# Routing of a two-level mixture of experts on one core: the first pair's weight slots released in two halves, logits in one operation, places read straight from TensorE's ranks, counts taken apart

## The reference, cut to what matters

```python
h = rmsnorm(x, g_ffn)
lg = h @ w_rg + b_rg                      # 4 group logits
g_onehot = one_hot(argmax(lg), 4)
le = (h @ w_re).reshape(..., 4, 8) + b_re # 32 expert logits
le_sel = sum(le * g_onehot[..., None], axis=-2)
tv, ti = top_k(le_sel, 2)                 # 2 of the 8 experts of the chosen group
gate = p_top * softmax(tv)                # spread over the 32 experts
for e in range(32):
    hid = silu(h @ w_e1[e]) * (h @ w_e3[e])   # 1024 -> 256
    y = y + gate[..., e:e+1] * (hid @ w_e2[e])  # 256 -> 1024
x = x + y
```

## Time and profile before

| what | us |
|---|---|
| time, median of 3 runs (lowest, highest) | 663.09 (662.82, 663.72) |
| time of the profiled execution | 663.22 |
| its span in the trace | 661.4 |
| TensorE busy | 621.0 |
| VectorE busy | 331.7 |
| ScalarE busy | 170.2 |
| GpSimd busy | 152.1 |

### The profile page before, as it was taken

How to read it: one execution, slowest core, us unless ns; L and a number is a source line. 1 busy time by engine, 2 the same in 40 slices (tenths; PEclk the granted TensorE clock), 3 DMA queues, 4 the chain that set the end, 5 groups by cost and what they waited for, 6 DMA issues and landing times.

```text
span 661.4 us, 9857 instructions
## 1 busy us (share of the span) xinstructions
PE 621.0 (94%) x3662; PEld 381.5 (58%) x3662; DVE 331.7 (50%) x878; ACT 170.2 (26%) x540; POOL 152.1 (23%) x341
## 2 busy tenths in 40 slices
PE   6999999999989889999999999997999999987886
PEld 5678876676545557776677756854344343333341
DVE  2162765878787997721123331477236335333333
ACT  4425223421558513232110001111121120120200
POOL 1497445733477963000000000000000000000000
PEclk9899999999999899999999999999999999997997
DMA  9763472221401072031289994077999999999993
GB/s 284 177 216 129 160 231 95 65 65 28 162 0 33 1 254 75 23 113 47 97 250 370 407 367 159 1 293 317 416 415 416 415 417 418 416 417 417 416 408 115
DMA packets 61681, 150.55 MB, mean 228 GB/s; under 512 B 12352, under 2 KB 40448, under 8 KB 53696
## 3 DMA queue, kind: packets, MB, share of 16 engines
q1 hardware_dynamic: 61632, 149.89, 61.2%
HBM read 147.12 MB, written 2.76 MB: 227 GB/s over the span
## 4 chain that ended last, share of the span: by engine, by line
PE 51%; DVE 7%; SPq 3%; DMA 3%; issue 2%; POOL 2%; ACT 1%; DVEq 0%
PE PS L811 18%; PE PS L1178 7%; PE PS L1087 6%; PE PS L819 5%; PE PS L1217 4%; PE PS L1207 4%; DMA E<-in_w_e 3%; SPq L700 3%; PE PS L932 1%; PE PS L955 1%; DVE X L2070 1%; PE PS L1139 1%; PE PS L1060 1%; SPq L704 1%; DVE rotB L1688 1%
## 5 line engine op out<-in xcount | busy, mean ns | idle before, releaser
L811 PE MATMUL PS<-hT,W 128*128 128x320 f32 x448 | 128.4, 442 | 1.1 <-issue 1.1
L811 PEld LDWEIGHTS PS<-hT,W 128*128 128x128 f32 x448 | 85.2, 193 | 39.0 <-issue 7.3
L1178 PE MATMUL PS<-E,xT 128*32 128x256 f32 x1024 | 61.5, 393 | 8.2 <-issue 7.2
L2142 POOL TENSOR_SCALAR means<-sums 128x4 f32<-128x4 f32 (+3 forms) x35 | 7.9, 227 | 224.5 <-ACT junk L1315 223.0
L1178 PEld LDWEIGHTS PS<-E,xT 128*32 128x32 f32 x1024 | 36.3, 114 | 37.6 <-issue 22.0
L1087 PE MATMUL PS<-h,S 128*128 128x512 f32 (+1 forms) x96 | 48.2, 625 | 0.7 <-DVE S L1929 0.7
L1217 PE MATMUL PS<-yb,WG 128*128 128x512 f32 (+1 forms) x96 | 42.8, 654 | 4.0 <-DVE X L2070 3.1
L819 PE MATMUL PS<-W,hT 128*128 128x256 f32 (+5 forms) x256 | 41.8, 353 | 1.6 <-ACT memT L1297 1.6
L2070 DVE TENSOR_TENSOR X<-X,PS 128x512 f32<-128x512 f32 (+1 forms) x48 | 33.0, 687 | 10.2 <-PE PS L1217 8.6
L819 PEld LDWEIGHTS PS<-W,hT 128*128 128x128 f32 (+1 forms) x256 | 31.5, 163 | 10.2 <-ACT memT L1297 1.8
L819 PE MATMUL PS<-W,mergedT 128*128 128x384 f32 (+3 forms) x192 | 35.8, 382 | 1.6 <-DVE mergedT L1838 1.6
(11 more groups left out here) (313 smaller groups left out, 952.4 us busy)
## 6 DMA issues: line engine op xcount, KB each, us to landing
E<-in_w_e SPq DMA_DIRECT2D x93, 1024.0 KB, 21.8
W<-in_w_in SPq DMA_DIRECT2D x7, 1536.0 KB, 7.3
W<-in_w_in SPq DMA_DIRECT2D x7, 1024.0 KB, 9.3
W<-in_w_mem_kv SPq DMA_DIRECT2D x4, 1024.0 KB, 6.0
W<-in_w_glu SPq DMA_DIRECT2D x4, 768.0 KB, 7.4
W<-in_w_out SPq DMA_DIRECT2D x2, 1536.0 KB, 14.8
E<-in_w_e SPq DMA_DIRECT2D x6, 512.0 KB, 18.8
X<-in_x_prompt SPq DMA_DIRECT2D x4, 512.0 KB, 5.2
```

The source lines that it names most:

```text
L811: ins = mm(out[:, 0:TOK], w[:, k, cols:cols + 128], rhs[:, k, :], start=(k == 0), stop=(k == kt - 1))
L1178: ins = mm(PS[r:r + B, 2 + par, 0:FF], xT[:, k, place_ + B * n:place_ + B * n + B], E13[slot][:, :, k, 128 * j:128 * j + 128], start=(k == ...
L2142: link(g_.tensor_scalar(means[0:rows_, n, 0:heads], sums[0:rows_, n, 0:heads], 1.0 / NORM_WIDTH[key[0]], EPS, ALU.mult, ALU.add))
```

## The change

Four edits.

1. **The weight slots of the first pair.** The loads of experts 7 and 8 are cut into halves over k. The first halves (k 0 to 3, 4 DMAs of 512 KB) are issued when `up(0)` has finished its step k = 3 (`first_half`), the second halves (4 more of 512 KB) at `ab_full`. `up` waits for both.
2. **Logits in one operation.** The router's columns are laid experts first, then groups, so that one operation writes 36 logits in place of two (4 and 32).
3. **Places straight from TensorE.** Each rank product gets a further product, `ones` of 32 rows by `iota`, which adds 32 times the expert's number. What `of_expert` picks is then already the place. `homes` goes from three small operations to two; the bound 32 times the expert plus 32 is computed in `experts`, and the plain rank is restored later by one operation ahead of `jcmp`.
4. **Counts apart.** The experts' counts are no longer accumulated beside the last ranks. `last_ranks` ends after one product, and three products into another bank follow (`counted`); VectorE copies them after the second half of `normed(2)`.

```diff
-            for p in range(PAIRS):
-                if 2 * p + UPS < NE:
+            for k0 in (0, KD // 2):
+                sp.wait_ge(s["first_half"] if k0 == 0 else s["ab_full"], 1)
+                for e in range(2):
+                    for n in range(2):
+                        sp.dma_start(E13[e][:, n, k0:k0 + KD // 2, :], e13_src[n][:, e + UPS, k0:k0 + KD // 2, :])\
+                            .then_inc(up_loaded[e] if k0 == 0 else s[f"rest{e}_loaded"], 16)
+            for p in range(PAIRS):
+                if p > 0 and 2 * p + UPS < NE:
...
             def first_ranks():
-                mm(PS[:, YB, 0:NE], const("upper"), both[:, 0, :], start=True, stop=True).then_inc(s["rank_full"], 1)
+                mm(PS[:, YB, 0:NE], const("ones", B), const("iota", B)[:, 0:NE], start=True, stop=False)
+                mm(PS[:, YB, 0:NE], const("upper"), both[:, 0, :], start=False, stop=True).then_inc(s["rank_full"], 1)
 
             def next_ranks():
-                mm(PS[:, YB, NE:2 * NE], const("upper"), both[:, 1, :], start=True, stop=False)
+                mm(PS[:, YB, NE:2 * NE], const("ones", B), const("iota", B)[:, 0:NE], start=True, stop=False)
+                mm(PS[:, YB, NE:2 * NE], const("upper"), both[:, 1, :], start=False, stop=False)
                 mm(PS[:, YB, NE:2 * NE], const("ones"), both[:, 0, :], start=False, stop=True).then_inc(s["rank_full"], 1)
                 for t in range(NT - 1):
-                    mm(PS[:, LAST_RANKS, 0:2 * NE], const("ones"), both[:, t:t + 1, :].broadcast_to([128, 2, NE]), start=(t == 0), stop=False)
+                    mm(PS[:, LAST_RANKS, 0:NE], const("ones"), both[:, t, :], start=(t == 0), stop=False)
+                mm(PS[:, LAST_RANKS, 0:NE], const("ones", B), const("iota", B)[:, 0:NE], start=False, stop=False)
 
             def last_ranks():
-                mm(PS[:, LAST_RANKS, 0:NE], const("upper", DEC), both[0:DEC, 2, :], start=False, stop=False)
-                mm(PS[:, LAST_RANKS, NE:2 * NE], const("ones", DEC), both[0:DEC, 2, :], start=False, stop=True).then_inc(s["rank_full"], 1)
+                mm(PS[:, LAST_RANKS, 0:NE], const("upper", DEC), both[0:DEC, 2, :], start=False, stop=True).then_inc(s["rank_full"], 1)
+                for t, (f, n) in enumerate(TILES):
+                    ins = mm(PS[:, YB, 0:NE], const("ones", n), both[0:n, t, :], start=(t == 0), stop=(t == NT - 1))
+                ins.then_inc(s["counted"], 1)
...
-                st.mark(V_.scalar_tensor_tensor(lg[0:n, t, 0:NG], src[0:n, 0:NG], r, brow[0:n, 0:NG], ALU.mult, ALU.add))
-                link(V_.scalar_tensor_tensor(lg[0:n, t, 8:40], src[0:n, NG:NG + NE], r, brow[0:n, NG:], ALU.mult, ALU.add), s["emptied_dve"])
+                link(V_.scalar_tensor_tensor(lg[0:n, t, 0:NE + NG], src[0:n, 0:NE + NG], r, brow[0:n], ALU.mult, ALU.add), s["emptied_dve"])
...
+                st.mark(V_.tensor_scalar(pos2[:, :, ts], ek2[:, :, ts], float(B), float(B), ALU.mult, ALU.add))
...
-                if ts.stop == NT:
-                    st.mark(V_.tensor_copy(n_, PS[:, LAST_RANKS, NE:2 * NE]))
                 link(of_expert(rank2[:, :, ts], ranks.rearrange("p (k t e) -> p k t e", k=1, e=NE), ts))
-                st.mark(V_.tensor_scalar(pos2[:, :, ts], rank2[:, :, ts], float(B), FAR, ALU.is_ge, ALU.mult))
-                link(V_.scalar_tensor_tensor(home[:, :, ts], ek2[:, :, ts], float(B), rank2[:, :, ts], ALU.mult, ALU.add))
-                link(V_.tensor_tensor(home[:, :, ts], home[:, :, ts], pos2[:, :, ts], ALU.add))
+                link(V_.tensor_tensor(home[:, :, ts], rank2[:, :, ts], pos2[:, :, ts], ALU.is_ge))
+                link(V_.scalar_tensor_tensor(home[:, :, ts], home[:, :, ts], FAR, rank2[:, :, ts], ALU.mult, ALU.add))
...
+            dve.wait_ge(s["counted"], 1)
+            st.mark(V_.tensor_copy(n_, PS[:, YB, 0:NE]))
...
+            link(V_.scalar_tensor_tensor(rank2, ek2, float(-B), rank2, ALU.mult, ALU.add))
```

More of the change, by code:

```diff
@@ L542, in build @@
             ov_w ov_chosen ov_gated ov_rows_full ov_rows_ready ov_weights_full ov_weights_ready ov_xt_full ov_xt_ready ov_ab ov_tanh ov_hid ov_ht_full ov_ht_ready ov_y_mm ov_y_dve ov_sum_full
-            ov_added ov_step ov_done stored pe_passed act_step dve_step pool_step dve_moe ov_half last_up_loaded last_down_loaded""".split()
+            ov_added ov_step ov_done stored pe_passed act_step dve_step pool_step dve_moe ov_half last_up_loaded last_down_loaded counted first_half rest0_loaded rest1_loaded""".split()
         s = {n: sem(n) for n in names}
@@ L710, in _ @@
             sp.wait_ge(s["y_skipped"], 4)
-            sp.dma_start(wr[:, :, 0:NG], a["w_rg"][0].rearrange("(p k) n -> p k n", k=KD)).then_inc(s["router_loaded"], 16)
-            sp.dma_start(wr[:, :, NG:], a["w_re"][0].rearrange("(p k) n -> p k n", k=KD)).then_inc(s["router_loaded"], 16)
+            sp.dma_start(wr[:, :, NE:], a["w_rg"][0].rearrange("(p k) n -> p k n", k=KD)).then_inc(s["router_loaded"], 16)
+            sp.dma_start(wr[:, :, 0:NE], a["w_re"][0].rearrange("(p k) n -> p k n", k=KD)).then_inc(s["router_loaded"], 16)
             sp.dma_start(gf[:], a["g_ffn"][0].rearrange("(p k) -> p k", k=KD)).then_inc(s["router_loaded"], 16)
-            sp.dma_start(brow[:, 0:NG], a["b_rg"][0].partition_broadcast(128)).then_inc(s["router_loaded"], 16)
-            sp.dma_start(brow[:, NG:], a["b_re"][0].rearrange("g e -> (g e)").partition_broadcast(128)).then_inc(s["router_loaded"], 16)
+            sp.dma_start(brow[:, NE:], a["b_rg"][0].partition_broadcast(128)).then_inc(s["router_loaded"], 16)
+            sp.dma_start(brow[:, 0:NE], a["b_re"][0].rearrange("g e -> (g e)").partition_broadcast(128)).then_inc(s["router_loaded"], 16)
             done(("mla", "OT", NT - 1))
@@ L1161, in up @@
                     pe.wait_ge(up_loaded[e % UPS], 32 * (e // UPS + 1))
+                    if UPS <= e < UPS + 2:
+                        pe.wait_ge(s[f"rest{e - UPS}_loaded"], 32)
                 pe.wait_ge(s["xt_ready"], 2 * (p // 2) + 1)
@@ L1170, in up @@
                     ins = up_products(k, [(2 * p + n) % UPS for n in range(2)], 64 * (p % 2), p % 2)
+                    if (p, k) == (0, KD // 2 - 1):
+                        ins.then_inc(s["first_half"], 1)
                 ins.then_inc(s["ab_full"], 1)
@@ L1877, in in_group @@
                 for t in tiles:
-                    at_ = st.mark(V_.max(r8[:, 0, t, :], lg[:, t, 0:8]))
+                    at_ = st.mark(V_.max(r8[:, 0, t, :], lg[:, t, NE:]))
                 st.after(at_)
                 for t in tiles:
-                    at_ = st.mark(V_.max_index(i8[:, 0, t, :], r8[:, 0, t, :], lg[:, t, 0:8]))
+                    at_ = st.mark(V_.max_index(i8[:, 0, t, :], r8[:, 0, t, :], lg[:, t, NE:]))
                 st.after(at_)
@@ L1885, in in_group @@
                                       rs[:, 0, ts, None].broadcast_to([128, nt, NG]), ALU.is_equal))
-                link(V_.tensor_tensor(prod[:, ts], lg[:, ts, 8:40].rearrange("p t (g e) -> p t e g", g=NG),
+                link(V_.tensor_tensor(prod[:, ts], lg[:, ts, 0:NE].rearrange("p t (g e) -> p t e g", g=NG),
                                       ex4[:, 2, ts, None, :].broadcast_to([128, nt, EPG, NG]), ALU.mult))
@@ L1977, in _ @@
             experts(only[2])
-            V_.tensor_tensor(ex4[:, 0], lg[:, :, 0:NG], r8[:, 0, :, 0:1].broadcast_to([128, NT, NG]), ALU.subtract)\
+            V_.tensor_tensor(ex4[:, 0], lg[:, :, NE:NE + NG], r8[:, 0, :, 0:1].broadcast_to([128, NT, NG]), ALU.subtract)\
                 .then_inc(s["logits_in"], 1)
```

## The result

The changed kernel takes **665.36 us** in the median (661.47 to 668.27, 22 executions), the kernel before it 663.17 beside it (661.60 to 664.16, 22 executions): a ratio of 1.0035, 95% interval 1.0018 to 1.0052. It is slower by 0.35%; the forecast was 662.6 with a range up to 664.0. The profiled execution took 666.93, its span 665.1 (before 663.22 and 661.4).

The account below looks back on a forecast made before the run. The prediction took the start of the unbroken expert-weight stream, set by expert 7's first load, to bound the kernel. Its terms, -1.83 + 0.66 + 0.60 - 0.14 - 0.10 - 0.07 + 0.07 + 0.3, gave -0.5 us: 662.6, range 661.0 to 664.0.

Parts of the forecast that it names:

- What bounds the kernel: Expert-weight stream: the end follows the first load of expert 7; each us earlier saves one, up to 2.4 us.
- The early release: Loads of expert 7: waiting for half of `up(0)` instead of all of it makes them 1.83 us earlier.
- Products and switches: TensorE's routing chain: three more small products cost 0.66 us, five more changes of form 0.60 us.
- Rival 1: TensorE's routing: new products are cheap, switches and perhaps products free; 661.3 to 662.0; chance 0.20.
- Logits: VectorE in the routing of tile 2: one operation in place of two saves 0.14 us.
- The terms of 0.07 and 0.10: VectorE, tile 2: counts copy off the chain saves 0.10; fewer `homes` operations save 0.07, the `experts` bound loses 0.07.
- The wait for the hidden rows: TensorE in pair 0: restoring the rank lengthens this wait from 3.03 to 3.3 us, with nothing at the end.
- Smaller transfers: Loads of experts 7 and 8: 4 MB in 4 KB rows at 409 GB/s instead of 425, 0.3 us later.
- rival 3: Half loads of experts 7 and 8: each pays its own start, +6 us, 668.6; chance 0.03.
- Rival 4: Tail: TensorE's clock falls one step earlier, ahead of the last half of the last up; 665; chance 0.08.
- rival 5: Tail: the clock stays up, gaining at least 0.9 us and some more in the sums; about 661; chance 0.04.

Follow-up runs that it names:

- h1: The kernel before with only the loads of experts 7 and 8 halved and the first halves released early; 662.66 us, ratio 1.0000.
- h2: The changed kernel with the loads of experts 7 and 8 whole and at `ab_full`, the other edits kept; 663.33 us, ratio 1.0013.
- h3: The kernel before with the loads of experts 7 and 8 cut into eight halves, all issued at `ab_full`; 664.34 us, ratio 1.0025.
- h12: The kernel before with experts 4 to 6 loaded in halves over k, in the middle of the routing; a single execution, 661.38 us.
- h13: The kernel before with eight unread 32-wide products (1.97 us) added ahead of `next_ranks`; 667.34 us, ratio 1.0054.
- h14: The kernel before with two unread wide products (512 and 384 columns, 1.77 us) added ahead of `next_ranks`; 664.07 us, ratio 1.0029.
- h15: The changed kernel with the three products preparing the last ranks moved from `next_ranks` to behind `route(2)`; 664.02 us, ratio 1.0020.
- h6: The changed kernel with one unread 512-wide product (1.05 us) added ahead of `next_ranks`; 665.16 us, ratio 1.0039.
- h5: The changed kernel unaltered, measured again; 665.72 us, ratio 1.0048 against the kernel before.
- h9: The changed kernel with four unread 32-wide products (1.01 us) added ahead of `next_ranks`; five counted times, ratio 1.0079.
- h8: The kernel before with the loads of experts 7 and 8 cut by partitions into eight 512 KB DMAs with 8 KB rows; 673.94 us, ratio 1.0168.

## Why the prediction was wrong

**What bounds the kernel: right.** The end moved by the start of the stream and its losses, and by nothing else: 1.97 + 1.76 is the 3.7 of the span. One reading was off without harm: from the issue to the first packet it is 1.0 us (453.42 behind 452.41 before, 455.36 behind 454.38 after), not 1.5; the bytes flow at full rate only somewhat later.

**The early release: right.** 1.83 was forecast, 1.7 measured in the profiles of h1 and of the changed kernel.

**Products and switches: right.** 1.26 was forecast. By the weight loads, the stretch from the transposes to the next `wout` unit, with `first_ranks` in it, went from 1.23 to 1.76 us, and the one from the next transposes to the product behind `next_ranks` from 1.92 to 2.71: together 1.32. Rival 1 fell with that. By the Trainium skill, "TensorEngine Tiling (Array Packing)", section Key Properties, a change of the tiling mode drains TensorE. The trace agrees: here such a change costs about 0.12 us each. Only the part in `next_ranks` is seen again at `up(0)` in h2 (+0.79, less the gains on VectorE, is the 0.56 measured there). The 0.53 of `first_ranks` lies ahead of that stretch. h2's profile reaches its start as early as before, but it is the earliest of its kind: the six profiles with the new `first_ranks` reach it at 433.4 to 435.3 (mean 434.2), the twelve with the old at 432.3 to 433.9 (mean 433.0). So the new ones do reach it later; the scatter of the stages ahead is too large to read its size from this. h2's ratio, 0.9 us with an interval from 0 to 1.8, fits it.

**Logits: right** (0.14 forecast), from 0.40 to 0.28 between the start of the operation and `MAX8`:

```profile
441.12 0.25 DVE L1879 SCALAR_TENSOR_TENSOR lg<-PS,rstd,brow 64x36 f32<-64x36 f32 x1 [2.87 <-PE PS L1066]
441.40 0.17 DVE L1892 MAX8 r<-lg 128x8 f32<-128x8 f32 x1
```

The terms of 0.07 and 0.10 are too small to be told apart. The wait for the hidden rows, said to grow from 3.03 to 3.3 us, was 2.67, and nothing hangs on it.

**"Smaller transfers ... I take 0.3 us later": the step that failed.** The term measured 1.7 (h3, h1) and 1.8 in the stream of the changed kernel. Its price of 409 GB/s came from a stretch near the end in which such transfers had been running for long, and it holds there. At the place of the change the stream starts anew behind a queue that has run dry, and there it is 236 to 340 GB/s for 8 us. I had given rival 3 only 0.03 because starts overlap in the running stream; its size (+6) was wrong, its direction right. The rule of the Trainium skill that the prediction weighed, "DMA: Bandwidth & Descriptors", section Bandwidth, batches of 1 MiB or more, was on the right side too, although h12 shows that size alone is not the cause. With 1.7 in place of 0.3 the sum is +0.9: 664.0, just the median of the 19 executions below 666, at the edge of the range and past it for a good part of them.

**A term that was missing.** Rival 4 had the clock fall one step earlier, but at the end, behind a wait. It fell in the routing, with TensorE never idle ahead of it, and costs 2.9 us in both profiles of the changed kernel: this was put at nothing. 15 of 34 executions lie above 666.9. That the added narrow products bring it on is shown by h13 against h14, and h15 and h6 agree. The two profiles of the changed kernel (666.93 and 668.31) and that of h13 (667.73) have the fall in the routing, and none of the others has; that the other executions of the upper group have it is inferred from their times. The rows gave a warning that I passed over: I priced each narrow product by its length and asked only whether it lies on the chain, not what it leaves TensorE doing. The tail, which the rival spoke of, is as before: 1.82 and 6.81 for the last down's second half and the sums. Where the clock falls later there (h1, h5) these are 1.11 and 4.72, but what follows takes longer instead: from the last down's second half to the end it is 12.7 us in the first kind (before, changed, h13) and 11.9 to 12.2 in all others but h6 (10.9). So rival 5's gain, said to be 0.9 and more, is about 0.6. By the Trainium skill, "TensorE: Matmul & The Clock Gate", section HAM oscillation, waits for DMAs bring the clock to half. The rows agree near the end, behind the wait of 3.04 us, and not in the routing, where no such wait stands ahead.

**What stays open.** Why a stream of half rows starts slowly. The records of single packets in the changed kernel's trace show 4 KB packets that take 159 ns each once the stream runs, but 189 to 262 ns in the mean of each window from 456 to 464, so some of them stall; the 8 KB packets before take an even 309 ns. On what they stall was not found. Why the clock falls in some executions and not in others is open too: h9, with more narrow products and no fall in its one profile, and h2, with hardly an upper group, aren't explained. The upper group lies 3.7 us above the lower one (medians 667.7 and 664.0), of which the fall in the routing explains 2.9; the 0.6 of the tail goes with it in two of the three profiles that have the fall.

## What to carry to other kernels

Price a transfer by a row of the same situation: a rate read in a full, long-running queue says nothing of the first microseconds after the queue was empty, and those are the ones that an early release is meant to win. Before putting small products on TensorE's chain, look at how long a run of narrow work they make, and read the times as a list and not as a median: two groups some 4 us apart were here the sign of a clock that falls in some of the executions. Where the times scatter as much as the effect, compare a stretch between two fixed events of the profiles: the stream separated whole loads from halves without an overlap, which the times did not. And a cheap reordering of products should be timed by itself first, since which column groups alternate can cost more than what it releases.

## What the runs showed of the hardware

- The granted clock fell to half with TensorE fully busy: in the changed kernel 0.2 us and 1.2 us behind a run of 64-wide and 32-wide products of 2.7 us, in h13 within such a run. With 1.77 us of 512-wide and 384-wide products added in place of 1.97 us of 32-wide ones it stayed at full. The fall is not in every execution, nor in the profile of h9.
- A small product takes 0.22 us whether 32 or 64 wide, and some 0.12 more where the number of rows changes, with 32 rows as with 64.
- Transfers of 512 KB with 4 KB rows, first into a queue that had run dry, ran at 236 to 385 GB/s for 6 to 8 us (after, h3, h12; in h9 at 205 to 244), at a DMA share of 0.86 to 1.00 (0.78 to 1.00 in h9), then at 408 to 422. With 8 KB rows it was 377 in the first full window, then 418 to 430 in the next four.
- Transfers into 64 of 128 partitions ran at 201 to 229 GB/s (h8), those into all of them at about 420.
- 32 products of 32 columns took 3.66 us going through four column groups in turn, 6.27 us alternating between two.
